# A two-layer hybrid trunk on one core: the modulation product moved from TensorE and GpSimd to VectorE, with turned weights and an opening by pairs of tiles

## The reference

```python
c_act = silu(c)                                   # c: (1, 1024)
for l in range(2):
    mod = c_act @ ada_w[l] + ada_b[l]             # 1024 x 6144, per layer
    sh1, sc1, g1, sh2, sc2, g2 = split(mod, 6)
    h = rmsnorm(x, norm1_w[l]) * (1 + sc1) + sh1  # x: (256, 1024)
    mix = token_mixer(h, ...)                     # conv module, state-space part, attention, gates
    x = x + g1 * mix
    h = rmsnorm(x, norm2_w[l]) * (1 + sc2) + sh2
    x = x + g2 * (swiglu(h) if l == 0 else moe(h))
out = rmsnorm(x, final_norm_w)
```

## Time and profile before

| | us |
|---|---|
| median of 3 runs | 1886.6 (1885.35 to 1887.86) |
| span of the profiled execution | 1888.6 |
| PE busy | 1778.0 (94%) |
| DVE busy | 483.9 (26%) |
| ACT busy | 276.5 (15%) |
| POOL busy | 353.6 (19%) |
| DMA | 541.92 MB, mean 287 GB/s |

### The profile page before, as it was taken

How to read it: one execution, slowest core, us unless ns; L and a number is a source line. 1 busy time by engine, 2 the same in 40 slices (tenths; PEclk the granted TensorE clock), 3 DMA queues, 4 the chain that set the end, 5 groups by cost and what they waited for, 6 DMA issues and landing times.

```text
span 1888.6 us, 28344 instructions
## 1 busy us (share of the span) xinstructions
PE 1778.0 (94%) x11337; PEld 1307.8 (69%) x11338; DVE 483.9 (26%) x1052; ACT 276.5 (15%) x567; POOL 353.6 (19%) x215
## 2 busy tenths in 40 slices
PE   7999999999999999999999989989999998999896
PEld 4888788778888788888885857565554443444443
DVE  1595535310000286322322001102100100101101
ACT  2104433010000210534011000000000100000001
POOL 2807241569998000000000000000000000000000
PEclk8999999999999999999989999979999999999999
DMA  9745464367765444445458979898998999999994
GB/s 397 259 156 201 151 232 139 129 251 281 266 246 194 177 145 152 134 145 168 178 208 365 416 286 401 346 419 350 418 414 337 412 421 417 419 418 418 416 421 178
DMA packets 86831, 541.92 MB, mean 287 GB/s; under 512 B 8752, under 2 KB 21072, under 8 KB 21840
## 3 DMA queue, kind: packets, MB, share of 16 engines
q1 hardware_dynamic: 67824, 490.24, 65.7%
q0 software_dynamic: 5760, 41.95, 6.0%
q10 hardware_dynamic: 13024, 6.82, 1.2%
HBM read 537.89 MB, written 1.08 MB: 285 GB/s over the span
## 4 chain that ended last, share of the span: by engine, by line
PE 84%; DMA 7%; issue 3%; SPq 2%; DVE 2%; ACT 2%; ACTq 0%; DVEq 0%
PE ps L799 22%; PE ps L1247 12%; PE ps L876 8%; PE ps L893 8%; PE ps L1395 6%; PE ps L1286 6%; PE ps L900 4%; PE ps L1416 3%; PE ps L1325 3%; DMA sq<-in_moe_units 3%; SPq L597 2%; DMA aring<-in_moe_units 2%; DMA misc<-in_moe_units 1%; PE ps L1357 1%; DMA proj<-in_ada_units 1%
## 5 line engine op out<-in xcount | busy, mean ns | idle before, releaser
L799 PE MATMUL ps<-hT,ring 128*128 128x256 f32 x1984 | 438.0, 382 | 1.0 <-ACT hT L1518 1.0
L799 PEld LDWEIGHTS ps<-hT,ring 128*128 128x128 f32 x1984 | 376.7, 191 | 56.1 <-issue 5.1
L701 POOL TENSOR_TENSOR aring<-aring,ccol 128x2048 f32<-128x2048 f32 x40 | 144.5, 3612 | 208.8 <-DVE scan L1941 65.8
L707 POOL TENSOR_TENSOR aring<-aring 128x1024 f32<-128x1024 f32 x80 | 151.3, 1892 | 6.3
L893 PE MATMUL ps<-hT,ring 128*128 128x256 f32 x672 | 146.7, 379 | 0.0
L1247 PE MATMUL ps<-ring,hT 128*64 128x256 f32 (+2 forms) x1152 | 131.7, 364 | 7.8 <-issue 5.6
L893 PEld LDWEIGHTS ps<-hT,ring 128*128 128x128 f32 x672 | 127.0, 190 | 16.9
L1247 PEld LDWEIGHTS ps<-ring,hT 128*64 128x64 f32 (+2 forms) x1152 | 75.0, 133 | 59.5 <-issue 37.9
L2286 DVE TENSOR_TENSOR proj<-proj,ps 128x256 f32<-128x256 f32 (+2 forms) x28 | 14.6, 521 | 352.5 <-PE ps L1247 352.5
L1926 DVE SCALAR_TENSOR_TENSOR misc<-cpad,par,misc 128x256 f32<-128x256 f32 x240 | 102.7, 507 | 0.0
L876 PE MATMUL ps<-proj,ring 128*128 128x256 f32 x384 | 83.2, 379 | 0.0
(11 more groups left out here) (399 smaller groups left out, 1969.0 us busy)
## 6 DMA issues: line engine op xcount, KB each, us to landing
ring<-in_moe_units SPq DMA_DIRECT2D x144, 1024.0 KB, 19.4
ring<-in_dense_units SPq DMA_DIRECT2D x121, 1024.0 KB, 5.0
aring<-in_moe_units SPq DMA_DIRECT2D x48, 1024.0 KB, 18.8
proj<-in_moe_units SPq DMA_DIRECT2D x48, 1024.0 KB, 20.2
aring<-in_ada_units POOLq DMA_DIRECT2D x40, 1024.0 KB, 6.6
extra<-in_moe_units SPq DMA_DIRECT2D x24, 1024.0 KB, 18.2
scan<-in_moe_units SPq DMA_DIRECT2D x24, 1024.0 KB, 21.2
misc<-in_moe_units SPq DMA_DIRECT2D x24, 1024.0 KB, 21.6
```

Of the source, the lines that this page charges most:

```text
L701: last = g.tensor_tensor(w, w, ccol[:, :].unsqueeze(2).broadcast_to([P, KT, 256]), ALU.mult)
L707: last = g.tensor_tensor(dst, w[:, 0:half_k, :], w[:, half_k:2 * half_k, :], ALU.add)
L799: last = mm(ps[:, n % 2, j * SEQ:(j + 1) * SEQ], wide(s)[:, k, j * P:(j + 1) * P], hT[:, k, :], start=(k == 0), stop=(k == KT - 1))
```

## The change

The modulation weights are stored turned: a unit is two halves of [128 outputs, 1024 inputs], so that an output's whole sum lies along one partition's row. DVE multiplies a half by silu(c), which lies broadcast in all partitions (`c_act`, 512 KB, loaded as such), sums along the row and starts from the bias, in one operation that leaves one column of the modulation. PE's products, column sums and transposes, ACT's copies and POOL's multiplications and additions for it are gone. POOL only starts 80 loads of half a unit, into three slots, and scales the normed tiles of layer 0's first norm. The opening goes by pairs of tiles: the units come in the order 4, 0, 5, 1, 6, 2, 7, 3, a factor is made for two tiles as soon as their two units are summed, and the first chunk of PE runs tile by tile. The first dense unit is asked for ahead of the last two modulation units. The bias columns are a transfer of their own.

```diff
-ADA_SLOTS = 2
+ADA_SLOTS = 3
+ADA_REST = ([(0, a) for a in (8, 9, 10, 11, 16, 17, 18, 19, 12, 13, 14, 15, 20, 21, 22, 23)]
+            + [(1, a) for a in (4, 5, 6, 7, 0, 1, 2, 3, *range(8, ADA_CHUNKS))])
-ADA_ORDER = (4, 5, 6, 7, 0, 1, 2, 3)
+ADA_ORDER = (4, 0, 5, 1, 6, 2, 7, 3)
...
+        HALF_AT = [30, 32] + [32 + 3 * T for T in range(1, 7)] + [50 + 2 * T for T in range(1, 16)]
...
+                if i == ADA_FIRST - 3:
+                    sp.dma_start(ring[:, 0, :], dense_units[0]).then_inc(full[0], 16)
...
+            for h in range(2):
+                if h == 0:
+                    pool.wait_ge(sd_s, 2)
+                g.tensor_tensor(sq[:, 4 * h:4 * h + 4, :], xT[:, 4 * h:4 * h + 4, :],
+                                rs[:, 2, :].unsqueeze(1).broadcast_to([P, 4, SEQ]), ALU.mult).then_inc(nx_s, 4)
+
+            pool.wait_ge(h_s, KT)
+            for h in range(ADA_HALVES):
+                if h >= ADA_SLOTS:
+                    pool.wait_ge(amod_s, h - ADA_SLOTS + 1)
+                l, a = ADA_REST[h // 2]
+                g.dma_start(aring[:, h % ADA_SLOTS, :],
+                            ada_units[l * ADA_CHUNKS + a].rearrange("p (c n) -> p c n", c=2)[:, h % 2, :]
+                            ).then_inc(afull[h % ADA_SLOTS], 16)
...
-                        if first and j == 0:
-                            pe.wait_ge(h_s, 2 * KT * l + k + 1)
...
+            def first_chunk(s, fill):
+
+                pe.wait_ge(full[s], fill)
+                for k in range(KT):
+                    pe.wait_ge(h_s, k + 1)
+                    for j in range(2):
+                        last = mm(ps[:, 0, j * SEQ:(j + 1) * SEQ], wide(s)[:, k, j * P:(j + 1) * P], hT[:, k, :],
+                                  start=(k == 0 and j == 0), stop=(k == KT - 1), skip_group_check=True)
+                last.then_inc(proj_s, 1)
...
-                        if g:
-                            ada_transpose(1, g - 1)
-                    for q in range(GD - 1, ADA_CHUNKS // 2):
-                        ada_transpose(1, q)
...
+            act.dma_start(c_act, c_rows[:, :]).then_inc(c_in_s, 16)
+            act.dma_start(par[:, 0:DEPTH * ROWS], par_cols[:, 0:DEPTH * ROWS]).then_inc(bias_s, 16)
             act.wait_ge(c_in_s, 16)
+            a_(c_act, c_act, ACT.Silu).then_inc(ccol_s, 1)
+            act.dma_start(par[:, DEPTH * ROWS:], par_cols[:, DEPTH * ROWS:]).then_inc(par_s, 16)
...
+            def ada_sum(w, l, col, dst):
+
+                return v.tensor_tensor_reduce(w, w, c_act, 1.0, pcol[:, l, R_ADA + col:R_ADA + col + 1], ALU.mult, ALU.add,
+                                              dst[:, col:col + 1])
+
+            def ada_unit(i):
+
+                dve.wait_ge(afirst[i], 16)
+                for c in range(2):
+                    ada_sum(ada_first[i][:, c, :], 0, 2 * ADA_ORDER[i] + c, modc).then_inc(afirst_s, 1)
+
+            def ada_halves(h0, h1):
+
+                for h in range(h0, h1):
+                    l, a = ADA_REST[h // 2]
+                    dve.wait_ge(afull[h % ADA_SLOTS], 16 * (h // ADA_SLOTS + 1))
+                    ada_sum(aring[:, h % ADA_SLOTS, :], l, 2 * a + h % 2, modn if l else modc).then_inc(amod_s, 1)
...
-                    rms_inverse(0)
+                    dve.wait_ge(bias_s, 16)
+                    dve.wait_ge(ccol_s, 1)
+                    ada_unit(0)
+                    ada_unit(1)
+                    ada_unit(2)
+                    rms_var(0)
+                    ada_unit(3)
+                    dve.wait_ge(sd_s, 1)
+                    v.reciprocal(rs[:, 2, :], rs[:, 1, :]).then_inc(sd_s, 1)
+                    for i in range(ADA_FIRST // 2):
+                        if i >= 2:
+                            ada_unit(2 * i)
+                            ada_unit(2 * i + 1)
+                        dve.wait_ge(afirst_s, 4 * i + 4)
+                        first_factor(i)
...
+                if l == 0:
+                    ada_halves(0, 8)
...
-                    if l == 0 and k and 3 + k < LATE:
-                        ada_reduce(0, 3 + k, modc)
+                    if l == 0:
+                        ada_halves(8 + k, 9 + k)
...
+                    if l == 0 and idx < 3:
+                        ada_halves(16 + 3 * idx, min(24, 19 + 3 * idx))
...
+                    if l == 0 and idx < 3:
+                        ada_halves(24 + 2 * idx, 26 + 2 * idx)
...
-                        if T % 2 == 0 and T > 2:
-                            ada_reduce(1, T // 2 - 2, modn)
-                    for q in range(GD - 2, ADA_CHUNKS // 2):
-                        ada_reduce(1, q, modn)
+                        ada_halves(HALF_AT[T], HALF_AT[T + 1])
```

More of the change, by code:

```diff
@@ L127, in pieces, with trunk @@
     return out
[L130 removed]
+def trunk(nc, x_cols, c_rows, par_cols, final_rows, ada_units, dense_units, moe_units, out):
     fp32, i32 = mybir.dt.float32, mybir.dt.int32
@@ L234, in trunk @@
         o_tm = proj[:, 24:32, :].rearrange("p (t a) n -> p t (a n)", t=TT)
-        eslot = ([aring[:, i, :] for i in range(ADA_SLOTS)] + [extra[:, :]]
+        eslot = ([aring[:, 2 * i:2 * i + 2, :].rearrange("p a n -> p (a n)") for i in range(2)] + [extra[:, :]]
                  + [ring[:, i, :] for i in range(SLOTS)]
@@ L672, in _ @@
             g.memset(cpad[:, :, :], 0.0).then_inc(cst_s, 1)
-            def ada_load(n):
-                i = n - ADA_FIRST
-                slot = (n + 1) % ADA_SLOTS
-                if i < ADA_SLOTS:
-                    pool.wait_ge(adam_s, ADA_FIRST)
-                else:
-                    pool.wait_ge(apool_s, i - ADA_SLOTS + 1)
-                g.dma_start(aring[:, slot, :], ada_units[n]).then_inc(afull[slot], 16)
-            steps = 0
-            for n in range(ADA_FIRST, ADA_FIRST + ADA_SLOTS):
-                ada_load(n)
```

187 lines of the change are left out of this document (39 added, 148 removed).

## The result

The changed kernel took 1873.94 us in the median of four runs (1871.03 to 1874.91), the kernel before 1887.12 (1885.35 to 1887.86) beside it: a ratio of 0.9922, 95% interval 0.9909 to 0.9935, or 13.2 us less. It is faster by more than the 0.2% that a measurement can tell, and lies inside the predicted range of 1859 to 1879; the gain that the sum forecast, 20.1 us, is 7 us larger than what came, and the time lies outside the 1861 to 1872 that the prediction gave the case of its sum.

What follows compares the result with a forecast made beforehand. The prediction took PE's matmuls to bound the kernel (84% of the chain). Its terms, 5.0 + 1.0 + 2.5 + 3.0 + 2.7 + 5.9 = 20.1 us off the median 1886.6, gave 1866.5 us, range 1859 to 1879.

Steps and rivals of the forecast that it cites:

- the case of its sum: Whole kernel: the summed gains of 20.1 us come about, giving 1861 to 1872 us; chance 0.56.
- The price of a half: DVE's multiplication and row sum over half a unit costs 1.3 us, with bounds 1.1 and 2.6.
- The rival of the double price: A half's sum on DVE costs twice the plain multiplication, 2.3 us: 1885.5 us, no change, or slower; chance 0.09.
- The opening: Start of the kernel: first chunk of PE ends at 39.5 us against 44.54, a gain of 5.0 us.
- 24.2 + 2 + 10.8 = 37.0: Opening: first factors' end, plus contention with POOL, plus eight more halves and two factors, puts the last factor at 37.0 us.
- as it has been running for more than 5 us by then: End of the first chunk: reason for taking 39.5 us out of 38.9 to 41.0, with PE at 2.4 GHz.
- the opening gives nothing: Opening: late DVE start, POOL and sums delaying each other, PE at 1.2 GHz for last tiles; 1871.6 to 1876; chance 0.20.
- The state's inputs and scores: Layer 0's state inputs and scores, where DVE ran beside POOL: gain 1.0 us, between 0 and 3.2.
- Between the last chunks: Six groups of four transposes leave PE's stream between the last chunks: gain 2.5 us, 3.5 at most.
- Last merge and output mix: Last merge without POOL beside it gains 3.0 us; output mix without transposes and a reduction wait gains 2.7.
- The feed-forward part: Nine groups of transposes at 0.44 us and 1.94 us at the end go: gain 5.9 us.
- The first eight halves: DVE sums ahead of the convolution, ending at about 69 us: no cost unless more than about 7 us later.

Runs made afterwards that it cites:

- the combined kernel: Changed kernel plus scaling of normed tiles on DVE and extra unread matmuls while PE waits in the opening and at both later norms: 1867.31 us, again 1863.08.
- set 2: Runs sharing one measurement of the kernel before: changed kernel with sums made twice 1877.51, without pairs 1875.68, the combined kernel 1867.31, changed kernel again 1872.18 us.
- set 1: Runs sharing one measurement of the kernel before: changed kernel with DVE scaling 1872.29, PE busy in opening 1870.15, at norms 1869.69, transposes put back 1879.46 us.

## Why the prediction was right in sign and too large

- **The price of a half.** Right: taken as 1.3 us, measured 1.28, 1.21 from start to start. It runs at the rate of the plain multiplication, and the second instruction takes 0.08 us. The rival of the double price falls. For this operation, which has two fp32 sources in SBUF and an accumulator, the trace does not agree with the point of the Trainium skill quoted there ("Vector Engine (DVE) Microarchitecture Reference", section "Points that are easy to get wrong"): no halving shows. The page names one instruction form, and no run tells whether this operation (CUSTOM_DVE_ANT_0 in the trace) is that form.
- **The opening** (5.0): mis-sized; it gave 0.6 in the profile of the changed kernel, and up to 3.5 in those where the clock was kinder. The steps that failed are "24.2 + 2 + 10.8 = 37.0" and the 2.5 us behind it. The last factor was done at 39.6, 2.6 later, and the chunk ended 4.35 behind it, 1.85 more: 4.4 of the 5.0. By terms: DVE began 0.8 earlier, and sixteen sums were 1.4 cheaper. It waited 0.9 for the third unit and 2.0 for the norm's sums; the sum had no term for these, and they took 6.64 on PE. The contention with POOL was 4.1, not 2: I chose the middle where the rule of the Trainium skill ("SBUF — State Buffer", section "Who interferes with whom") allowed all of it, and the trace agrees with the rule (4.1 against the 3.8 that I had worked out for the whole). POOL's two operations took 6.6 us there and not 3.8; what they take alone no run shows. Last, "as it has been running for more than 5 us by then" was wrong: PE had idled for 3 us, and ran the last tiles at 1.2 GHz. Even the bounds had too little for that: they put 1.0 and 1.7 behind the factor, where the prediction's own rates give 0.5 for ACT and 3.5 for two tiles. The experiment with DVE's scaling shows the contention, the one with PE kept busy the norm's sums and DVE's wait, each in its own rows; the combined kernel takes them away together: 5.4 us.
- **The rival "the opening gives nothing"** (0.20, 1871.6 to 1876) is what happened in the changed kernel's profiles (0.6 both times) and by its median, through two of its three causes: the sums and POOL hold one another up, and PE is at 1.2 GHz for the last tiles. The third, a late start of DVE, did not come. Its reason for the clock was not quite right either: the granted clock was at 1.00 again from 34 to 40 us and fell once more behind the idle 3 us. That the total stayed in the stated range owes to the range having covered this rival; the case of the sum, 1861 to 1872, missed it. I had argued that it needs all bounds at once; two waits that the sum didn't have made up for the missing one.
- **The state's inputs and scores** (1.0): the chain moves from 0.63 us early at the second chunk to 1.60 at the scores, 0.97.
- **Between the last chunks** (2.5): 2.48 (1.60 to 4.08).
- **Last merge and output mix** (5.7): 6.64 (4.08 to 10.72), without a gap in 69.07 us. Only the two groups of transposes in it, 0.88, are shown by a run; the rest is read from the chains.
- **The feed-forward part** (5.9): right for the transposes; 5.9 from 389.44 on, after the stretch behind norm 2 had lost 0.95.
- **A term that I had not**: the clock behind the norms. It took back 0.95 and 1.3 us. Both lie within what the eight profiles vary by, so they are not the change's doing; with PE kept busy the two places are worth 2.6 and 3.0 us.
- **The first eight halves** were done at 76.9 us, not at about 69, and the convolution began 6.9 us later than before. That cost PE nothing, as forecast, though they ended more than the 7 us later at which I had seen the convolution set the pace: the second part of it was done at 147.4, where it had been 153.7, and ACT took it up at 158.0. DVE waited 44.8 us in all for transfers, 19 times, off the path.
- **The experts' part** moved as a whole: 1236.0 and 1234.2 against 1237.8, within the 1234 to 1240 of all profiles but the one with doubled sums.

In sum the terms outside the opening were forecast as 15.1, and came to 16.0 before the clock took 2.25 back.

## What to carry to other kernels

When work is moved off a bound engine, look at what that engine's idle time does to its clock. Filling 3 to 4 us of waiting with matmuls that nobody needs gave 1.4 to 3.0 us at each norm, as much as one of the smaller terms of the change. Place them so that the clock has not fallen before they begin, and so that they end before the real work is ready: six of them in the opening ran at the lower rate and held PE up for about 1.1 us. The reduction of one row by a matrix was well placed on DVE here, with the weights turned: it is hidden behind PE as long as DVE's share between two of its hand-overs to PE stays below PE's time for them (three halves, 3.6 us, were; doubled, they were not). A large GpSimd operation beside DVE's stream on the path holds DVE up (4.1 us for two), so eight multiplications by DVE itself (2.8 us) were cheaper.

## What the runs showed of the hardware

- A DVE operation with two fp32 sources of 128x1024 and a sum along the row: 1.28 us, 1.21 from start to start, 0.08 us for the read of the sum.
- The same operation beside a GpSimd multiplication of 128x1024: 3.35 us, and the GpSimd one 3.3.
- The norm's sums, 16 records, are PE's first work in the changed kernel. They took 5.5 to 6.6 us, and 3.72 when other matmuls ran before them, 3.69 in the kernel before. The windows of the changed kernel show the granted clock at 1.00 all the while, with 6 matmul records in a window in which the combined kernel has 11 (also at 1.00):

```profile
16.00:18.00 2.00, 2.00 (x6) 1.58 (x5) 2.00 (x3) 0.52 (x1) 0.00 (x0) 1.00 1.00 418
```

  The combined kernel's own first matmuls are as slow (7 records from 6 to 8 us, at 1.00). So the granted clock alone doesn't tell PE's rate in its first work. What does is open.
- The same program on the chip twice, in two sets: medians 1867.31 and 1863.08, with ranges of 1.7 us each. A difference of 4 us between sets says nothing here. Within set 2, medians 3.5 and 4.9 us from the changed kernel's had ranges that did not touch its own; within set 1, medians 0.5 to 2.6 us apart had ranges that overlap.
